# Four PSUM banks dealt anew, a batch's output scaled a slot earlier, and the probabilities turned in two halves

## The chip, the core and the metric

The kernel runs on one core of a Trainium2 chip. The metric is the device time of one execution in microseconds (us). The core's engines are TensorE (PE in the profile, its weight loads PEld), VectorE (DVE), ScalarE (ACT), GpSimd (POOL) and SyncE (SP), which issues nearly all transfers.

## The reference, cut to what matters

One step of a one-layer decoder trunk: 256 prompt tokens and 8 sequences (batches 0 to 7) of 8 new tokens, 320 columns in all.

```python
z = rmsnorm(x) @ w_in                    # 2048 -> 5120, split into q, k, v, u, h, gb, gc
# sample tokens, for each batch b: 8 queries x 16 heads against the cached keys (1280 of
# the 2048 positions are ever reached) and the 8 new ones, three dilated patterns merged
s = q @ k.T * HEAD_DIM**-0.5; s = where(valid, s, NEG)
p = exp(s - max(s)); o_att = (p @ v) / sum(p)
# prompt tokens: the same for 8 pairs of heads; besides it
h = associative_scan(exp(a*dt), u @ B); y = gelu(h @ C + D*u); y = y * sigmoid(y @ w_glu + b)
y_conv = gb * conv3(gc * h_in)
x = x + concat(rmsnorm(o_att), rmsnorm(y), rmsnorm(y_conv)) @ w_out
x = x + (silu(xn @ w_gate) * (xn @ w_up)) @ w_down     # xn = rmsnorm(x)
```

## The kernel before

All activations lie feature-major, [128 features, 320 tokens]. Each float32 weight is split into a high and a low part (`whi` by ScalarE, `wlo = raw - whi` by VectorE), and each product is made of three matmuls of 320 columns. The weights come in units of 512 KB, each 24 matmuls of TensorE.

The first 96 units (80 of `w_in`, then 16 of `w_out`) are the *slots* s = 0 to 95, and everything else of the layer is woven into them by slot numbers. On TensorE a slot is: the unit, with the calls of `middle(s)` inside it, then `end(s)`. On ScalarE and VectorE each slot holds, among other work, the split of unit s+2: ScalarE's copy waits for the end of unit s, so it begins where TensorE begins `end(s)`. Every engine runs its own list in order; what a slot's list holds late waits for what it holds early. After slot 95 only dense work is left, the loops over `w_gate`/`w_up` and `w_down` (from 587 us on).

Sample attention of batch b runs from slot START_OF[b] = 36, 42, 48, 54, 60, 66, 72, 78:

- slots +0 to +3: TensorE `scores(b, i)` into bank 6, at the end of the slot; VectorE `mask_scores(b, i)` adds the mask on the way into `sall` and takes the maxima. It stands ahead of VectorE's split of unit s+2 in the same slot.
- +4, +5: ScalarE spreads the maxima over the four groups of 32 partitions (`spread_maxima`, `spread_bias`, VectorE's `maxima` between them) and makes the exponentials of `sall` in place, groups 0 and 1 in slot +4, groups 2 and 3 in +5, with their sums in `psums`.
- +6 (TURN): VectorE `turn_probabilities(b)` transposes `sall` in 32x32 blocks into `ptk`, one instruction of 1408 elements a partition, after the ten value products of batch b-1 have read `ptk` (`v_used`). In slot +6 the scores of batch b+1 begin.
- +7 to +11 (VALUES): TensorE `values(b, j)`, ten products into bank 4, at the ends of the slots (1, 1, 1, 3 and 4 of them; two a slot for batch 7), and after the tenth `sum_probabilities(b)`, 4 tiny matmuls with the matrix `fold` that add the sums of the four partition groups.
- +11: VectorE `inverse_sums(b)`, a reciprocal out of bank 4.
- +12 (OUTPUT): ScalarE `scale_output(b)`: bank 4 times the reciprocal into `osb`, in its list behind the split of unit s+2. TensorE `turn_output(b)` waits for it and transposes `osb` back into bank 4, the last of the three kinds of work in `end(s)`: scores, values, turn. ScalarE `move_output(b)` takes the result away. Batches 0 and 1 (LATE) keep their output and turn it in slots 58 and 62, by way of bank 7.

Beside that: in slots 24 to 65 the state-space scan, 16 steps in 5 parts on VectorE. TensorE `project(i)`, in the middle of a slot, gives its input in two banks: 4 and 5 for i = 1, 3, 5, else 6 and 7. `read_out` takes four steps together into bank 5 (`y`, in slots 39, 50, 58 and 66), which VectorE's `scan_output` reads. In slots 66 to 82 there is prompt attention, a pair of heads in two slots: scores in banks 6 and 7 in the middle of the even slots (`prompt_masks` on VectorE), transposes into 6 and 7 at the end of the odd ones, values and output in bank 5. In 71 to 74 there are also the gate products in bank 5; slots 76 and 83 hold the sums of squares of two of the norms.

`fill(bank, key)` lets TensorE wait, ahead of each use of a bank, until the bank's last user in the order of the slots has been read. The function `fills(s)` writes that order down; for the banks of this change:

```python
def state_bank(i):
    return 4 if i < PAIRED and i % 2 else 6
...
"x": lambda: ("x_moved", key[1] + 1),
"score": lambda: ("s_masked", KS * key[1] + key[2] + 1) if key[2] < KS - 1 else ("new_masked", key[1] + 1),
```

So `project(10)` in slot 52 waits for the mask of batch 2's last scores (slot 51), `project(11)` in 55 for that of scores (3, 0), and `project(15)` in 63 for that of scores (4, 2), for all of them used bank 6.

Of the kernel before, what the change touches and what calls it, by code (L numbers as in the profile page):

```python
# [40 lines left out]
P = 128  # L41
# [169 lines left out]
def build(nc, a, o):  # L211
    with ExitStack() as ctx:
# [96 lines left out]
        psums = upper.take("psums", [P, DEC_BATCH, 4])  # L309
        fold = upper.take("fold", [P, 32])  # L310
# [36 lines left out]
        q_zero q_ready k_used s_masked s_max s_spread s_top s_bias p_exp p_turned new_masked fold_ready vn_zero  # L347
        p_sums s_sum v_used vn_done vn_moved
# [70 lines left out]
        def state_bank(i):  # L419
            return 4 if i < PAIRED and i % 2 else 6  # L420
# [14 lines left out]
        def fills(s):  # L435

            middle, end = [], []
            for i in range(ST):
                if scan_slot(i, 4) + 2 == s and i % 4 == 3:
                    middle.append((5, ("y", i // 4)))  # L440
            for i in projected(s):
                middle += [(state_bank(i), ("x", i)), (state_bank(i) + 1, ("x", i))]
# [22 lines left out]
            if s == VN_SLOT:  # L465
                end.append((7, ("vn", 0)))
            for b in range(LATE):
                if s == LATE_SLOTS[b]:
                    end.append((7, ("late", b)))
                if s == LATE_SLOTS[b] + 1:  # L470
                    end.append((7, ("turn", b)))
# [193 lines left out]
        def _(act):  # L665
# [70 lines left out]

            def exponent(b, groups):
                act.wait_ge(S["s_bias"], 4 * b + 4)
                for g in groups:
                    act.activation(sall[:, g, :], sall[:, g, :], ACT.Exp, bias=sbias[:, g:g + 1], scale=SCALE,  # L740
                                   accum_out=psums[:, b, g:g + 1]).then_inc(S["p_exp"], 1)
# [8 lines left out]
            def move_output(b):  # L750

                act.wait_ge(S["o_turned"], TURNS.index(b) + 1)
                bank = 7 if b < LATE else 4
# [48 lines left out]
            for s in range(SLOTS):  # L802
# [14 lines left out]
                for i in projected(s):  # L817
                    act.wait_ge(S["x_proj"], i + 1)
                    bank = state_bank(i)

                    if i > 1:
                        act.wait_ge(S["x_rot"], i - 1 if i <= PAIRED else i)
                    act.activation((xs if bank == 6 else xs_odd)[:], ps[:, bank:bank + 2, 0:NT], ACT.Copy).then_inc(S["x_moved"], 1)
# [42 lines left out]
                if s == VN_SLOT:  # L866
                    act.wait_ge(S["vn_done"], 1)
                    act.wait_ge(S["vn_zero"], 1)
                    for e in range(2):
                        act.activation(vn[0:64, 512 * e:512 * e + 512], ps[64 * e:64 * e + 64, 7, :], ACT.Copy).then_inc(S["vn_moved"], 1)  # L870
# [117 lines left out]
        def _(dve):  # L988
# [71 lines left out]
            def mask_scores(b, i):  # L1060

                if i == 0:
                    if b:
                        dve.wait_ge(S["p_turned"], b)
# [4 lines left out]
                v.tensor_tensor_reduce(out=sall[:, i, 0:KQ], in0=ps[:, 6, 0:KQ], in1=mask[:], scale=1.0, scalar=-3e38,  # L1069
# [9 lines left out]
                v.tensor_tensor(fresh, ps[own, 6, KQ:KQ + P].rearrange("p (a n) -> p a n", n=32), valid, ALU.add).then_inc(S["new_masked"], 1)  # L1079
# [15 lines left out]
            def turn_probabilities(b):  # L1095

                dve.wait_ge(S["p_exp"], 4 * b + 4)
                if b:
                    dve.wait_ge(S["v_used"], KEY_TILES * b)
# [4 lines left out]
                v.transpose(ptk[:].rearrange("p a n -> p (a n)"), sall[:].rearrange("p a n -> p (a n)")).then_inc(S["p_turned"], 1)  # L1104
                dve.wait_ge(S["p_turned"], b + 1)
# [3 lines left out]
            def inverse_sums(b):  # L1109
                dve.wait_ge(S["p_sums"], b + 1)  # L1110
                v.reciprocal(rsum[:, b:b + 1], ps[:, 4, 2 * P:2 * P + 1]).then_inc(S["s_sum"], 1)

            def scan(i, part):

                c_, s_ = (tab[:, i % 2, j:j + 1, :].to_broadcast([P, 2, NT]) for j in range(2))
                if part == 0:
# [3 lines left out]
                    x = xs if state_bank(i) == 6 else xs_odd  # L1120
# [43 lines left out]
            def scan_output(it):  # L1164
                dve.wait_ge(S["c_done"], 4 * it + 4)
                v.scalar_tensor_tensor(out=z[:, ZU + it, :], in0=z[:, ZU + it, :], scalar=vec[:, V_D + it:V_D + it + 1], in1=ps[:, 5, 0:NT],
# [66 lines left out]
            for s in range(SLOTS):  # L1233
# [24 lines left out]
                for b in batches(s, TURN):  # L1258
                    turn_probabilities(b)
# [72 lines left out]
                if s == START_OF[0] - 3:  # L1332
                    dve.wait_ge(S["early_done"], 1)
                    dve.wait_ge(S["ident_in"], 16)
# [858 lines left out]
```

## Time and profile before

| | us |
|---|---|
| median of 3 runs (lowest, highest) | 1539.41 (1535.3, 1539.87) |
| the profiled execution, its own time | 1536.41 |
| its span, first to last instruction | 1534.6 |
| busy: TensorE, VectorE, ScalarE, GpSimd | 1493.9, 842.2, 598.0, 218.6 |
| mean granted TensorE clock | 0.990 |

TensorE is busy for 97% of the span. Its matmuls are pipelined and their ends are modelled, so "busy" is not "at its peak". Times in the views are counted from the start of the span; a slot is about 5 to 9 us long in the stretch of slots 36 to 95, which lies between 141 and about 540 us.

### The profile page before, as it was taken

The page shows a single profiled execution, that of the slowest core. Times are in us where ns is not written, and L with a number is a line of the kernel's source. Part 1 is how long each engine was busy: PE and PEld are TensorE (multiplying, and loading weights), DVE is VectorE, ACT ScalarE, POOL GpSimd, SP SyncE. Part 2 cuts the span into 40 slices and gives each one's busy share as a digit, 9 for nine tenths or more (in the row PEclk, how much of TensorE's full clock was granted, in tenths as well). Part 3 has the DMA queues.
Part 4 walks back from the last instruction along what each step waited for, and adds up shares of the span by engine and source line. Part 5 has one row for each costly group of instructions (what it writes and reads, how often), then busy time and mean ns, then how long its engine had stood idle before and what let it go on. Part 6 is the DMA issues. An engine that isn't in the chain of part 4 may idle for free.

```text
span 1534.6 us, 27971 instructions
## 1 busy us (share of the span) xinstructions
PE 1493.9 (97%) x11431; PEld 1428.3 (93%) x11431; DVE 842.2 (55%) x1086; ACT 598.0 (39%) x883; POOL 218.6 (14%) x317
## 2 busy tenths in 40 slices
PE   9999998989989999999999999999999999999997
PEld 9998777778767899999999999999999999999997
DVE  7669899974467667544444444444444433333434
ACT  6333443437455354333333333333333433333332
POOL 7873344400440000000000000000000000000100
PEclk9999999999999999999999999999999999999999
DMA  7556798999779344444444444444444444444442
GB/s 265 190 168 220 277 377 308 346 338 372 270 262 369 125 152 151 146 147 148 148 150 150 150 150 150 149 146 147 148 149 150 151 151 151 151 144 152 145 152 109
DMA packets 93271, 296.41 MB, mean 193 GB/s; under 512 B 9728, under 2 KB 11008, under 8 KB 92800
## 3 DMA queue, kind: packets, MB, share of 16 engines
q1 hardware_dynamic: 92608, 294.10, 55.3%
q8 instruction: 63, 1.03, 0.3%
q10 hardware_dynamic: 576, 1.08, 0.2%
q14 instruction: 24, 0.20, 0.0%
HBM read 289.06 MB, written 5.43 MB: 192 GB/s over the span
## 4 chain that ended last, share of the span: by engine, by line
PE 84%; DVE 11%; ACT 3%; issue 2%; DMA 0%; SPq 0%; DVEq 0%; ACTq 0%
PE ps L2080 20%; PE ps L2079 20%; PE ps L2078 20%; PE ps L1924 5%; PE ps L1962 2%; PE ps L1926 2%; DVE wlo L1037 2%; PE ps L1968 2%; PE ps L1963 2%; PE ps L1775 1%; PE ps L1760 1%; PE ps L2029 1%; PE ps L2031 1%; PE ps L2030 1%; DVE tm L1122 1%
## 5 line engine op out<-in xcount | busy, mean ns | idle before, releaser
L1391 DVE TENSOR_TENSOR wlo<-raw,whi 128x1024 fp32r<-128x1024 f32 x264 | 325.3, 1232 | 519.9 <-ACT whi L914 519.7
L914 ACT ACTIVATE whi<-raw 128x1024 fp32r<-128x1024 f32 x264 | 279.9, 1060 | 606.2 <-PE ps L2080 601.7
L2080 PE MATMUL ps<-xh,wlo 128*128 128x320 f32 x1400 | 432.6, 309 | 0.0
L2078 PE MATMUL ps<-xh,whi 128*128 128x320 f32 x1400 | 432.6, 309 | 0.0
L2079 PE MATMUL ps<-xl,whi 128*128 128x320 f32 x1400 | 432.6, 309 | 0.0
L2078 PEld LDWEIGHTS ps<-xh,whi 128*128 128x128 f32 x1400 | 262.8, 188 | 0.0
L2079 PEld LDWEIGHTS ps<-xl,whi 128*128 128x128 f32 x1400 | 262.8, 188 | 0.0
L2080 PEld LDWEIGHTS ps<-xh,wlo 128*128 128x128 f32 x1400 | 262.8, 188 | 0.0
L2078 PE MATMUL ps<-hh,whi 128*128 128x320 f32 x696 | 215.1, 309 | 0.0
L2079 PE MATMUL ps<-hl,whi 128*128 128x320 f32 x696 | 215.1, 309 | 0.0
L2080 PE MATMUL ps<-hh,wlo 128*128 128x320 f32 x696 | 215.1, 309 | 0.0
L689 ACT ACTIVATE whi<-raw 128x1024 fp32r<-128x1024 f32 x110 | 116.2, 1057 | 188.8 <-PE ps L1924 89.6
L1037 DVE TENSOR_TENSOR wlo<-raw,whi 128x1024 fp32r<-128x1024 f32 x110 | 138.4, 1258 | 77.0 <-ACT whi L689 76.2
L1687 POOL TENSOR_TENSOR sq_last<-sq_last 128x1280 f32<-128x1280 f32 x2 | 5.9, 2972 | 1008.1 <-ACT sq_last L670 1008.1
L1924 PE MATMUL ps<-xh,whi 128*128 128x320 f32 x472 | 145.4, 321 | 0.0
L1926 PE MATMUL ps<-xl,whi 128*128 128x320 f32 x472 | 140.8, 311 | 0.0
L2079 PEld LDWEIGHTS ps<-hl,whi 128*128 128x128 f32 x696 | 130.7, 188 | 0.0
L2080 PEld LDWEIGHTS ps<-hh,wlo 128*128 128x128 f32 x696 | 130.7, 188 | 0.0
L2078 PEld LDWEIGHTS ps<-hh,whi 128*128 128x128 f32 x696 | 130.7, 188 | 0.0
L1924 PEld LDWEIGHTS ps<-xh,whi 128*128 128x128 f32 x472 | 89.4, 189 | 10.0 <-issue 7.7
L1962 PE MATMUL ps<-xh,whi 128*128 128x320 f32 x280 | 90.9, 332 | 0.0
L1926 PEld LDWEIGHTS ps<-xl,whi 128*128 128x128 f32 x472 | 89.6, 190 | 0.2
(336 smaller groups left out, 1836.7 us busy)
## 6 DMA issues: line engine op xcount, KB each, us to landing
raw<-in_w_gu SPq DMA_DIRECT2D x176, 512.0 KB, 3.3
raw<-in_w_dn SPq DMA_DIRECT2D x88, 512.0 KB, 3.3
raw<-in_w_in SPq DMA_DIRECT2D x78, 512.0 KB, 5.2
kv<-in_cv SPq DMA_DIRECT2D x64, 512.0 KB, 7.1
kv<-in_ck SPq DMA_DIRECT2D x32, 768.0 KB, 6.3
kv<-in_ck SPq DMA_DIRECT2D x32, 512.0 KB, 6.9
raw<-in_w_out SPq DMA_DIRECT2D x32, 512.0 KB, 3.4
raw<-in_cv SPq DMA_DIRECT2D x16, 512.0 KB, 7.8
```

The costliest lines, as they stand in the source:

```text
L689: act.activation(whi[:, u % SPL, :], raw[:, raw_place(u), :], ACT.Copy).then_inc(S["w_hi"], 1)
L914: act.activation(whi[:, j % SPL, :], raw[:, j % RAW, :], ACT.Copy).then_inc(S["w_hi"], 1)
L1037: v.tensor_tensor(wlo[:, u % SPL, :], raw[:, raw_place(u), :], whi[:, u % SPL, :].bitcast(F32), ALU.subtract) \
L1391: v.tensor_tensor(wlo[:, j % SPL, :], raw[:, j % RAW, :], whi[:, j % SPL, :].bitcast(F32), ALU.subtract) \
L1924: last = t_.matmul(ps[:, b0 + n, 0:NT], src[:, u % SPL, w], xh[:, k, :], start=False, stop=False)
L1926: t_.matmul(ps[:, b0 + n, 0:NT], whi[:, u % SPL, w], xl[:, k, :], start=False, stop=False)
L1962: t_.matmul(out, whi[:, u % SPL, w], xh[:, k, :], start=first, stop=False)
L1963: t_.matmul(out, whi[:, u % SPL, w], xl[:, k, :], start=False, stop=False)
L1968: last = t_.matmul(out, wlo[:, u % SPL, w], xh[:, k - 1 + kk, :], start=False, stop=j == units - 1 and kk == 1)
L2078: t_.matmul(out, whi[:, slot, w], ah[:, k, :], start=(k == 0), stop=False)
L2079: t_.matmul(out, whi[:, slot, w], al[:, k, :], start=False, stop=False)
L2080: last = t_.matmul(out, wlo[:, slot, w], ah[:, k, :], start=False, stop=(k == 2 * units - 1))
```

## The change

1. **Banks.** Scores go to bank 7 in place of 6. From i = 6 on the scan's input goes to banks 5 and 6 in place of 6 and 7. The second and third read-out (`y` 1 and 2, slots 50 and 58) go to bank 7, the others stay in 5. The new keys' and values' turn (`vn`) and the late batches' work go from bank 7 to 6.
2. **Sums.** `sum_probabilities`, its 4 matmuls a batch and `fold` are gone. In slot +7 ScalarE copies the four groups' sums side by side (`spread_sums`, 4 small copies); in +8 VectorE reduces them and takes the reciprocal; in +9 ScalarE deals the result out again (`deal_sums`, 4 small copies).
3. **Scaling.** `scale_output(b)` moves from slot +12 to +11, where it waits for the tenth value product of the same slot. In slot +12 `turn_output(b)` becomes the first work of `end(s)`, ahead of scores and values.
4. **Turn in halves.** VectorE transposes groups 0 and 1 at the end of slot +5 (after the exponentials of these two and `v_used` of batch b-1), ahead of the scan parts of that slot, and groups 2 and 3 in slot +6 in the place of the whole.

```diff
         def state_bank(i):
-            return 4 if i < PAIRED and i % 2 else 6
+            if i >= PAIRED:
+                return slice(5, 7)
+            return slice(4, 6) if i % 2 else slice(6, 8)
+
+        def y_bank(it):
+
+            return 7 if it in (1, 2) else 5
...
-                    end.append((6, ("score", b, step)))
+                    end.append((7, ("score", b, step)))
...
+            def spread_sums(b):
+
+                act.wait_ge(S["p_exp"], 4 * b + 4)
+                if b:
+                    act.wait_ge(S["s_sum"], b)
+                for j in range(4):
+                    act.activation(sums_at[0:32, j, :], psums[32 * j:32 * j + 32, b % 2, :], ACT.Copy).then_inc(S["p_sums"], 1)
+
+            def deal_sums(b):
+
+                act.wait_ge(S["s_sum"], b + 1)
+                for g in range(4):
+                    act.activation(rsum[32 * g:32 * g + 32, b:b + 1], sums_all[0:32, g:g + 1], ACT.Copy).then_inc(S["s_inv"], 1)
...
             def scale_output(b):
                 act.wait_ge(S["v_used"], KEY_TILES * (b + 1))
-                act.wait_ge(S["s_sum"], b + 1)
+                act.wait_ge(S["s_inv"], 4 * b + 4)
...
                 for b in batches(s, OUTPUT):
-                    scale_output(b)
                     if b >= LATE:
                         move_output(b)
+                for b in batches(s, VALUES + 4):
+                    scale_output(b)
...
+                for b in batches(s, VALUES):
+                    spread_sums(b)
+                for b in batches(s, VALUES + 2):
+                    deal_sums(b)
...
-            def turn_probabilities(b):
-
-                dve.wait_ge(S["p_exp"], 4 * b + 4)
-                if b:
-                    dve.wait_ge(S["v_used"], KEY_TILES * b)
+            def turn_probabilities(b, half):
+
+                dve.wait_ge(S["p_exp"], 4 * b + 2 * half + 2)
+                two = slice(2 * half, 2 * half + 2)
+                if half == 0:
+                    if b:
+                        dve.wait_ge(S["v_used"], KEY_TILES * b)
+                    v.transpose(ptk[:, two].rearrange("p a n -> p (a n)"), sall[:, two].rearrange("p a n -> p (a n)")).then_inc(S["p_turned"], 1)
+                    return
...
             def inverse_sums(b):
-                dve.wait_ge(S["p_sums"], b + 1)
-                v.reciprocal(rsum[:, b:b + 1], ps[:, 4, 2 * P:2 * P + 1]).then_inc(S["s_sum"], 1)
+
+                dve.wait_ge(S["p_sums"], 4 * b + 4)
+                if b:
+                    dve.wait_ge(S["s_inv"], 4 * b)
+                step(v.tensor_reduce(sums_all[0:32], sums_at[0:32].rearrange("p j g -> p g j"), AX.X, ALU.add))
+                v.reciprocal(sums_all[0:32], sums_all[0:32]).then_inc(S["s_sum"], 1)
...
                 for b in batches(s, 4):
                     maxima(b)
-                for b in batches(s, VALUES + 4):
+                for b in batches(s, VALUES + 1):
                     inverse_sums(b)
+                for b in batches(s, TURN - 1):
+                    turn_probabilities(b, 0)
...
             def end(s):
 
+                for b in batches(s, OUTPUT):
+                    if b >= LATE:
+                        turn_output(b)
...
-                for b in batches(s, OUTPUT):
-                    if b >= LATE:
-                        turn_output(b)
```

## Rows read from the trace of the kernel before

**Rows 1.** The page: the chain that ended last, by engine.
```profile
PE 84%; DVE 11%; ACT 3%; issue 2%; DMA 0%; SPq 0%; DVEq 0%; ACTq 0%
```

**Rows 2.** Waits of TensorE, whole span: total, times, longest, us.
```profile
PE ps L1800 <- ACT osb L748: 13.3, 6, 4.4
PE ps L1724 <- DVE smax L1069: 4.5, 2, 2.5
...
PE ps L1724 <- DVE sall L1079: 2.5, 1, 2.5
```

**Rows 3.** Busy us (instructions) by stretch: PE, PEld, DVE, ACT, POOL; clock, DMA share, GB/s.
```profile
130.00:257.00 127.00, 117.41 (x1225) 98.95 (x1225) 116.26 (x193) 51.84 (x123) 53.33 (x57) 0.99 0.84 301
257.00:286.00 29.00, 29.00 (x313) 22.75 (x314) 24.52 (x43) 9.81 (x21) 8.13 (x8) 0.94 0.86 320
286.00:312.00 26.00, 23.36 (x271) 19.15 (x270) 25.35 (x40) 12.20 (x37) 13.71 (x12) 1.00 0.96 353
312.00:333.00 21.00, 20.73 (x221) 16.45 (x221) 14.89 (x29) 8.38 (x24) 0.00 (x0) 0.92 0.87 323
333.00:378.00 45.00, 43.02 (x476) 35.49 (x474) 21.73 (x69) 26.37 (x71) 0.00 (x0) 1.00 0.97 365
```

**Rows 4.** Timeline of TensorE: start, duration, us; brackets: its idle time, and for what.
```profile
338.84 0.41 PE L1800 MATMUL ps<-ident,osb 128*128 128x128 f32 x2 [1.75 <-ACT osb L748]
...
386.39 0.41 PE L1800 MATMUL ps<-ident,osb 128*128 128x128 f32 x2 [2.54 <-ACT osb L748]
...
441.41 0.66 PE L1800 MATMUL ps<-ident,osb 128*128 128x128 f32 x2 [4.35 <-ACT osb L748]
...
484.18 0.41 PE L1800 MATMUL ps<-ident,osb 128*128 128x128 f32 x2 [2.06 <-ACT osb L748]
...
514.34 0.66 PE L1800 MATMUL ps<-ident,osb 128*128 128x128 f32 x2 [2.19 <-ACT osb L748]
```

**Rows 5.** TensorE alone by stretch: busy us, granted clock, DMA share, GB/s.
```profile
312.00:317.00 5.00, 4.73 (x35) 0.66 1.01 404
336.00:342.00 6.00, 4.25 (x54) 1.00 1.02 384
386.00:392.00 6.00, 5.61 (x30) 0.72 0.72 232
438.00:446.00 8.00, 4.59 (x24) 0.57 0.63 199
482.00:486.00 4.00, 1.95 (x14) 1.00 1.03 415
514.00:518.00 4.00, 3.66 (x16) 0.57 0.38 131
```

**Rows 6.** Timeline of TensorE and VectorE in slot 78.
```profile
435.77 1.29 PE L1760 MATMUL ps<-kv,qst 128*32 128x192 f32 x32 [1.68 <-issue]
...
436.14 0.08 DVE L1179 DVE_READ_ACCUMULATOR2_ANT pmax<- 128x1 f32 x1
```

**Rows 7.** Timeline of TensorE and VectorE in slots 47, 50 and 63.
```profile
204.64 1.93 PE L1775 MATMUL ps<-kv,ptk 128*32 128x256 f32 x32
...
224.59 1.29 PE L1760 MATMUL ps<-kv,qst 128*32 128x192 f32 x32
...
228.65 0.55 DVE L1166 SCALAR_TENSOR_TENSOR z<-z,vec,ps 128x320 f32<-128x320 f32 x1
...
312.27 1.04 PE L1724 MATMUL ps<-z,bt 32*128 32x320 f32 x4 [2.48 <-DVE smax L1069]
```

**Rows 8.** Small operations: duration ns min/median/max, first and last start us.
```profile
L1104 DVE STREAM_TRANSPOSE ptk<-sall x8: 1603/1641/1645, 178.1 to 481.6; 128x1408 f32<-128x1408 f32 x8
...
L1103 DVE STREAM_TRANSPOSE ptk_late<-sall x2: 313/314/314, 177.8 to 214.2; 128x128 f32<-128x128 f32 x2
...
L729 ACT ACTIVATE quads<-smax x32: 188/203/206, 167.4 to 472.2; 32x4 f32<-32x4 f32 x32
...
L1088 DVE TENSOR_REDUCE sbias<-quads x8: 158/163/170, 168.9 to 473.3; 32x4 f32<-32x16 f32 x8
```

More of the change, by code:

```diff
@@ L439, in fills @@
                 if scan_slot(i, 4) + 2 == s and i % 4 == 3:
-                    middle.append((5, ("y", i // 4)))
+                    middle.append((y_bank(i // 4), ("y", i // 4)))
             for i in projected(s):
-                middle += [(state_bank(i), ("x", i)), (state_bank(i) + 1, ("x", i))]
+                middle += [(bank, ("x", i)) for bank in range(8)[state_bank(i)]]
             for r in prompt_pair(s, 0):
@@ L465, in fills @@
             if s == VN_SLOT:
-                end.append((7, ("vn", 0)))
+                end.append((6, ("vn", 0)))
             for b in range(LATE):
                 if s == LATE_SLOTS[b]:
-                    end.append((7, ("late", b)))
+                    end.append((6, ("late", b)))
                 if s == LATE_SLOTS[b] + 1:
-                    end.append((7, ("turn", b)))
+                    end.append((6, ("turn", b)))
             return middle, end
@@ L752, in move_output @@
                 act.wait_ge(S["o_turned"], TURNS.index(b) + 1)
-                bank = 7 if b < LATE else 4
+                bank = 6 if b < LATE else 4
                 for e in range(2):
@@ L818, in _ @@
                     act.wait_ge(S["x_proj"], i + 1)
-                    bank = state_bank(i)
                     if i > 1:
                         act.wait_ge(S["x_rot"], i - 1 if i <= PAIRED else i)
-                    act.activation((xs if bank == 6 else xs_odd)[:], ps[:, bank:bank + 2, 0:NT], ACT.Copy).then_inc(S["x_moved"], 1)
+                    act.activation((xs_odd if i < PAIRED and i % 2 else xs)[:], ps[:, state_bank(i), 0:NT], ACT.Copy).then_inc(S["x_moved"], 1)
                 if s + 3 >= U_IN:
@@ L1119, in scan @@
                     dve.wait_ge(S["x_moved"], i + 1)
-                    x = xs if state_bank(i) == 6 else xs_odd
+                    x = xs_odd if i < PAIRED and i % 2 else xs
                     step(v.tensor_tensor(tm[:, 0:2], x[:], c_, ALU.mult), wait=False)
@@ L1258, in _ @@
                 for b in batches(s, TURN):
-                    turn_probabilities(b)
+                    turn_probabilities(b, 1)
                 for step_ in range(KS):
@@ L1720, in project @@
                 for plane, src in enumerate((z[:, ZU:ZU + NC, :], zr)):
-                    fill(state_bank(i) + plane, "x", i)
+                    bank = range(8)[state_bank(i)][plane]
+                    fill(bank, "x", i)
                     row = 32 * ((i + 2 * plane) % 4)
                     q = slice(row, row + 32)
-                    last = t_.matmul(ps[:, state_bank(i) + plane, 0:NT], bt[q, plane, i // 4, :], src[q, i // 4, :], start=True, stop=True,
+                    last = t_.matmul(ps[:, bank, 0:NT], bt[q, plane, i // 4, :], src[q, i // 4, :], start=True, stop=True,
                                      tile_position=(row, 0))
@@ L1759, in scores @@
                         for j in range(4):
-                            last = t_.matmul(ps[32 * j:32 * j + 32, 6, 64 * c0:64 * c1], qst[:, b % 2, 2 * i + half, :],
+                            last = t_.matmul(ps[32 * j:32 * j + 32, 7, 64 * c0:64 * c1], qst[:, b % 2, 2 * i + half, :],
                                              keys[:, :, half, :, j, :], start=(half == 0), stop=(half == 1), tile_position=(0, 32 * j))
                 last.then_inc(S["k_used"], 1)
-            def sum_probabilities(b):
-                pe.wait_ge(S["fold_ready"], 1)
-                pe.wait_ge(S["p_exp"], 4 * b + 4)
-                for g in range(4):
-                    last = t_.matmul(ps[32 * g:32 * g + 32, 4, 2 * P:2 * P + 1], fold[:], psums[:, b, g:g + 1], start=True, stop=True,
-                                     tile_position=(0, 32 * g))
-                last.then_inc(S["p_sums"], 1)
             def weigh(bank, turned, vals, start, stop):
@@ L1789, in values @@
                 weigh(4, ptk[:, :, 32 * j:32 * j + 32], kv_place(n), j == 0, j == KEY_TILES - 1).then_inc(S["v_used"], 1)
-                if j == KEY_TILES - 1:
-                    sum_probabilities(b)
             def turn_output(b):
-                bank, src = (4, osb) if b >= LATE else (7, osb_late[:, b, :])
+                bank, src = (4, osb) if b >= LATE else (6, osb_late[:, b, :])
                 if b >= LATE:
```

49 lines of the change are left out of this document (24 added, 25 removed).

## The prediction

> **What bounds the kernel now.** I read the page first. The chain that ended last runs over TensorE for 84% of the span and over VectorE for 11% [rows 1]. So time is to be had in two ways only: where TensorE stands idle or runs at its slow clock, and in the stretch where VectorE leads. Next I read the waits of TensorE [rows 2]. The largest by far is `osb`: six turns of an output wait for ScalarE's `scale_output`, 13.3 us in all. Three projections of the scan wait 4.5 + 2.5 = 7.0 us for VectorE's masks, because they share a bank with the scores. These four kinds of row are what the change is aimed at.
>
> Whether an idle microsecond is worth one depends on the stretch [rows 3]. From 130 to 257 us and from 286 to 312 VectorE is busy for 116.3 of 127 and 25.4 of 26 us: there VectorE paces, and TensorE's waits are TensorE waiting to be slow enough. From 257 to 286 and from 312 on it is the other way: TensorE is busy for 29.0 of 29 and 20.7 of 21 us, VectorE has 4.5 and 6.1 us free, and from 333 on about half. Five of the six `osb` waits lie in that late part, 1.75, 2.54, 4.35, 2.06 and 2.19 us long, 12.9 together [rows 4].
>
> The third thing read is the granted clock around these waits [rows 5]. Behind the wait that ended at 386.39 it averages 0.72 over 6 us, that is (1 - 0.72) x 6 x 2 = 3.4 us at 1.2 GHz instead of 2.4. Behind the ones at 514.34 and 312.27 it is 0.57 over 4 and 0.66 over 5 us: 3.4 us each too. Around 441.41 it is 0.57 over 8 us: 6.9 us slow, of which some 4 fall after TensorE goes on. Behind the waits of 1.75 and 2.06 us the clock stayed at 1.00. A slow stretch of 3.4 us does 1.7 us of work, so it costs 1.7 us more than the idle time in front of it.
>
> The Trainium skill's page "TensorE: Matmul & The Clock Gate", section "Part 1: The HAM clock gate", says that the slow clock is the default and that sustained activity releases it. The rows agree on the two levels.
>
> **The change part by part.**
>
> *Scaling a slot earlier, the turn first in its slot.* The product that `scale_output` needs is done at the end of slot +11, ScalarE scales it there, and the turn comes a whole unit later. All five late waits go. What ScalarE now waits for is `v_used`: it stands for at most the time of the value products less its own split copy. Behind it are queued the exponentials 2 and 3 of the next batch, which VectorE wants a slot later, and the prompt's probabilities, which come after the values in TensorE's list anyway. So I cost that wait at nothing, 0.5 us a batch if VectorE should be waiting. Gain 12.9 us. The clock: the stretches behind 386.39 and 514.34 go, 2 x 1.7 = 3.4 us.
>
> *What is late next, in slot 78.* There TensorE waits twice. Before the `osb` wait of 4.35 it stood 1.68 us at the scores, put down to "issue" [rows 6]; by the times this is VectorE's prompt masks (the fourth ended at 436.22 us; the second about 0.55 earlier, just before the scores' start at 435.77). Scores in bank 6 needed two of the masks; in bank 7 they need all four: +0.55. VectorE also makes the new first half of the turn in slot 77, ahead of the norm and of these masks: +0.9 (below). So this wait grows to about 3.1 us, 1.4 us lost, and at that length I expect the clock to fall behind it as it did behind 2.54, so the 2 us of slow work around 441 are not won. In the other even slots the fourth mask is done before the scores come, and I take 0; above 0.5 us each for five slots is the bound.
>
> *Halves of the transpose.* 1408 elements take 1641 ns, 128 take 314 [rows 8]: 1.037 ns an element and 181 ns fixed. A half of 704 costs 911 ns, two 1822: +0.18 us a batch. Between 0 (the fixed part hidden under its neighbour) and 0.36. Its wait for `v_used` of batch b-1 falls where VectorE is, by then, behind its split of the same slot; in the scan what is queued behind it are the scan parts and the next slot's masks.
>
> The page "VectorE: DVE Perf Modes" of the Trainium skill, section "The TRN2 errata", speaks against cutting an instruction up: a fixed cost is paid per instruction, some 150 cycles as it measured, which is 0.16 us by its clock. The rows give 0.18; by the page the halves would cost 8 x 0.16 = 1.3 us of VectorE's time in all instead of 1.4.
>
> *Sums.* VectorE: one more small reduce, 163 ns. ScalarE: 8 small copies of 203 ns, 1.6 us a batch; it has half of its time free from 333 on [rows 3], and the results are wanted two slots later: 0, or 1.6 us a batch if ScalarE led. TensorE loses 4 matmuls a batch; they lie in the gap it leaves anyway between tiled and full matmuls, so 0, at most 0.2 us each.
>
> *Banks, in the stretch to 333 us.* (a) The waits of projections 10, 11 and 15 go. Only the last lies where TensorE takes the lead: VectorE is free for 6.1 us after 312, so 2.48 us of idle time and 1.7 of slow clock come back: -4.2. The other two are worth something only between 257 and 286, where VectorE itself waited on TensorE: of its 4.5 us free there I take 2.5. (b) Read-out 1 now lies in bank 7, so scores (2, 2) must wait for `scan_output`. TensorE began them at 224.59; VectorE's `scan_output` ran at 228.65 to 229.20 [rows 7]. TensorE will stand for some 4.6 us, after which its clock falls. VectorE, which leads here, then waits for the scores (1.3 us long) before it can mask them, and about 1 us more in the next slot, since TensorE comes back at its slow clock: +2.3. (c) VectorE's 0.18 + 0.16 us for four batches: +1.4. Sum: -4.2 - 2.5 + 2.3 + 1.4 = -3.0.
>
> *Transfers.* None is added, but from 286 to 378 they run at a share of 0.87 to 0.97 and 323 to 365 GB/s; 404 and 415 GB/s over 4 to 5 us is the most the views show [rows 3, 5]. At 410 the 32.4 MB of these 92 us take 79 us, so the 5 to 6 us that I take out here fit, with bursts left over. I take 0.
>
> Sum: -12.9 - 3.4 + 1.4 - 3.0 = -17.9. The profiled execution took 1536.4, so 1518.5. The median of the runs stands 3.0 above that execution; I put half of it on: **1520 us**.
>
> **Rivals.**
>
> *A. The forecast.* 1520, its own range 1513 to 1527.
>
> *B. TensorE gains in the scan too.* If VectorE's lead is looser than its busy share says, the other two projection waits (4.5 us) and their slow stretches (3.4) come back in full: with the 2.5 already taken 1520 - 5.4 = about 1515, and with (b) unpaid as well 1512. Against it: 116 of 127 us busy.
>
> *C. Read-out 1 (and 2, slot 58) costs more.* TensorE stands 4.6 us with VectorE behind it, at the slow clock; if VectorE loses the whole of it, as much in slot 58, and 1.7 us of slow clock, that is 10.9 in place of 2.3: 1529. For it: VectorE leads there and every loss counts.
>
> *D. Something else is late in the prompt slots.* ScalarE's list or the transfers keep TensorE back where `osb` did. If the transfers give back all that is won up to 378 us, what is left are the four waits after it (11.1 us), their clock (3.4) and the 1.4 of slot 78: 1536.4 - 13.1 + 1.5 = 1525; if ScalarE's exponentials and table loads set slots 72 and 78, nothing much is left: 1536, no change. For it: 0.97 of DMA; against it: no wait for a transfer shows in the list.
>
> *E. Slower: VectorE blocked by the first half.* It waits for the ten value products of batch b-1, the last four of which take 1.93 us behind the unit [rows 7], about 2.3 with the new values' product; were VectorE always there early, that is 2.3 us of it a batch, and where a split or a mask behind it is late, as much for TensorE plus 1.7 us of clock: 4 x 8 = 32 us, 1520 + 32 = 1552. It decides once a batch loses 3.0 us of path (24 us in all). Against it: in the scan VectorE comes 2 us and more after the products, later it has half its time free.
>
> *F. The change doesn't do what it says:* the new scaling is itself late by a slot. It would need ScalarE a whole slot behind: 1539.
>
> **How the numbers follow.** Chances: A 0.50, B 0.08, C 0.14, D 0.16 (half of it with no gain), E 0.06, F 0.06. The range takes A, C, the better half of D and the nearer part of B: 1511 to 1532. A measurement here can tell 0.3%, 4.6 us, from no change. Faster: A + B + C + half of D = 0.80. Same: half of D and F with some of E's small end, 0.13. Slower: 0.07.
>
> **What would show it.** In the profile after: no wait of TensorE for `osb`, and the turn right behind each unit in slots 66 to 90; `scan_output` named as what scores (2, 2) wait for, 4 to 5 us, in slot 50; the wait at the scores of slot 78 grown to about 3 us; the granted clock at 1.00 around the turns of slots 72 and 90; two transposes of about 0.9 us a batch; VectorE at 312 us no earlier than 3 us before its old time. The forecast is wrong if VectorE's chain to 312 us grows by more than 3 us, or if a new row of ScalarE, VectorE or a transfer above 5 us appears among TensorE's waits.

## The result, and the profile after

The changed kernel takes 1517.03 us (median of 4 runs, 1515.17 to 1518.3), beside 1538.13 us for the kernel before on the same chip (4 runs, 1535.3 to 1539.87): a ratio of 0.9864, 95% interval 0.9844 to 0.9884. The forecast was 1520, its range 1511 to 1532. The profiled execution took 1515.17 us, its span 1513.3 at a mean clock of 0.997; before it was 1536.41 and 1534.6 at 0.990. So 21.2 us went, where the sum of the prediction had 17.9.

The page of the kernel after, the chain that ended last by engine, beside [rows 1]:

```profile
PE 85%; DVE 8%; ACT 3%; POOL 2%; issue 1%; DMA 0%; DVEq 0%; ACTq 0%
```

TensorE's waits in the kernel after (total, times, longest, us), beside [rows 2]:

```profile
PE ps L1793 <- DVE smax L1093: 4.1, 3, 1.8
PE ps L1793 <- DVE z L1198: 3.6, 1, 3.6
PE ps L1793 <- issue: 2.6, 1, 2.6
...
PE ps L1739 <- DVE sqc L1332: 1.6, 1, 1.6
PE ps L1770 <- DVE smax L1093: 0.9, 1, 0.9
```

No row of `osb` is left and none of a projection. What is new are four single waits: 3.6 us of scores for `scan_output` (`z`, slot 50), 2.6 us of scores in slot 78, 1.6 us of a norm's sums of squares in slot 83 (0.4 us before), and 0.9 us of read-out 1 in slot 50, which in bank 7 has to follow the mask of slot 49's scores.

Busy time by stretch in the kernel after (columns as in [rows 3]):

```profile
130.00:257.00 127.00, 116.95 (x1206) 98.30 (x1205) 114.52 (x188) 54.39 (x137) 52.13 (x53) 0.99 0.82 290
257.00:286.00 29.00, 29.00 (x323) 22.91 (x322) 27.98 (x54) 12.28 (x34) 11.17 (x12) 1.00 0.97 374
286.00:312.00 26.00, 26.00 (x299) 21.11 (x301) 25.37 (x40) 13.72 (x40) 13.19 (x12) 1.00 0.99 367
312.00:333.00 21.00, 21.00 (x241) 16.52 (x233) 17.84 (x44) 11.00 (x38) 0.00 (x0) 1.00 1.04 400
333.00:378.00 45.00, 44.90 (x475) 36.35 (x475) 21.41 (x70) 32.08 (x87) 0.00 (x0) 1.00 0.97 370
```

TensorE alone, in windows behind the five late turns and behind the two waits at scores (columns as in [rows 5]; the row from 428 begins 4.9 us behind slot 78's turn, the wait at the scores lies between them):

```profile
226.00:236.00 10.00, 6.38 (x62) 0.83 0.66 238
...
330.00:336.00 6.00, 6.00 (x71) 1.00 1.03 372
376.00:382.00 6.00, 6.00 (x65) 1.00 0.71 241
428.00:434.00 6.00, 6.00 (x72) 1.00 0.77 261
466.00:472.00 6.00, 5.77 (x49) 1.00 1.02 410
494.00:500.00 6.00, 6.00 (x43) 1.00 0.40 135
...
426.00:434.00 8.00, 7.99 (x113) 1.00 0.60 204
```

Between 257 and 286 us VectorE, which had 4.5 us free before, is now busy for 27.98 of 29: both engines are full. The clock, 0.94 and 0.92 in the second and fourth stretch before, is 1.00. TensorE stops for none of the five late turns, and the clock stays up behind them.

The scores of slots 50 and 78, and two of the turns, in the timelines of TensorE and VectorE after (start, duration, us; brackets: idle time before, and its releaser), beside [rows 4, 6, 7]:

```profile
229.51 0.55 DVE L1198 SCALAR_TENSOR_TENSOR z<-z,vec,ps 128x320 f32<-128x320 f32 x1
230.12 1.81 PE L1793 MATMUL ps<-kv,qst 128*32 128x192 f32 x32 [3.62 <-DVE z L1198]
231.97 0.49 DVE L1093 CUSTOM_DVE_ANT_0 sall<-ps,mask 128x320 f32<-128x320 f32 x1 [1.91 <-PE ps L1793]
...
330.46 0.38 PE L1822 MATMUL ps<-ident,osb 128*128 128x128 f32 x2
466.52 0.38 PE L1822 MATMUL ps<-ident,osb 128*128 128x128 f32 x2
...
425.84 0.08 DVE L1211 DVE_READ_ACCUMULATOR2_ANT pmax<- 128x1 f32 x1
426.01 1.29 PE L1793 MATMUL ps<-kv,qst 128*32 128x192 f32 x32 [2.56 <-issue]
```

The turns follow with no idle time in brackets. In slot 50 TensorE begins its scores 0.06 us after `scan_output` ends, at the slow clock (32 products in 1.81 us, not 1.29), and VectorE then waits 1.91 us for them. In slot 78 the scores begin 0.09 us after the fourth mask's maximum is read out (425.84 + 0.08), as the prediction had it; but behind this wait the clock is 1.00.

The small operations after (duration ns min/median/max, first and last start us), beside [rows 8]:

```profile
L1126 DVE STREAM_TRANSPOSE ptk<-sall x8: 899/905/911, 174.9 to 465.8; 128x704 f32<-128x704 f32 x8
L1132 DVE STREAM_TRANSPOSE ptk<-sall x8: 869/905/912, 179.1 to 466.7; 128x704 f32<-128x704 f32 x8
...
L1142 DVE TENSOR_REDUCE sums_all<-sums_at x8: 159/163/169, 191.2 to 480.1; 32x4 f32<-32x16 f32 x8
...
L750 ACT ACTIVATE sums_at<-psums x32: 187/203/205, 180.4 to 477.2; 32x4 f32<-32x4 f32 x32
L756 ACT ACTIVATE rsum<-sums_all x32: 182/200/203, 195.3 to 483.2; 32x1 f32<-32x1 f32 x32
```

To see where the 21 us went, one event that both kernels have is followed: the start of VectorE's `wlo` of each unit (unit s+2 is split in slot s). Each number below is such a start in the timeline, us. "Banks alone", "scaling late" and "no banks" are experiments 10, 1 and 4; "three edits" is experiment 9.

```
unit   before    after   banks   scaling    no    three
                         alone    late     banks  edits
  36   138.81   139.03   139.33   138.66   138.76  138.34
  51   221.44   222.30   221.97   221.92   222.01  220.91
  56   256.75   259.89   259.82   259.54   257.55  256.01
  59   277.32   276.18   276.46   275.83   276.05  272.35
  65   319.69   315.35   315.53   314.95   319.96  312.00
  68   338.37   333.13   333.62   333.16   338.61  329.78
  69   344.48   337.48   339.73   339.27   342.97  334.14
  74   385.92   378.82   380.73   380.61   384.77  375.46
  75   396.74   385.60   389.99   392.71   391.56  382.24
  80   439.51   429.00   432.62   436.10   435.10  424.24
  81   450.83   434.89   443.56   447.20   440.98  430.29
  83   464.98   448.70   457.59   461.23    455.12  444.10
  84   470.92   455.52   463.53   468.05   461.94  450.92
  90   503.44   486.01   496.05   500.55   492.46  481.91
  93   520.90   499.61   512.08   516.54   506.05  495.51
 110   581.37   560.09   572.55   577.01   566.53  555.98
```

The difference before to after grows in steps: +0.9 us at unit 51, +3.1 at 56 (slot 50), -1.1 at 59, -5.2 at 68 (slots 55 and 63), -7.0 at 69 (slot 66), -11.1 at 75 (slot 72), -10.5 at 80, -15.9 at 81 and -16.3 at 83 (all slot 78), back to -15.4 at 84 (slot 83), -17.4 at 90 (slot 84) and -21.3 at 93 (slot 90). From there to the end nothing changes.

One execution of a kernel differs from another, too. Kernels 2, 6, 7 and 8 below have the same instructions as after up to slot 48, and they reach unit 51 at 221.85, 221.76, 221.84 and 221.81 us, some 0.5 us sooner than after. A step of half a microsecond in this table is therefore not told from scatter.

### The profile page after: what moved, and what is told of

The parts are those of the page before. It is cut to its first block, busy times and chain, and to the rows that moved or that the text cites. A ratio compares the mean times of both kernels' runs of the same rounds, so it can differ in the third digit from the quotient of the medians.

```text
span 1513.3 us, 27929 instructions
## 1 busy us (share of the span) xinstructions
PE 1485.5 (98%) x11367; PEld 1419.5 (94%) x11367; DVE 841.6 (56%) x1101; ACT 609.5 (40%) x947; POOL 219.9 (15%) x317
## 4 chain that ended last, share of the span: by engine, by line
PE 85%; DVE 8%; ACT 3%; POOL 2%; issue 1%; DMA 0%; DVEq 0%; ACTq 0%
PE ps L2102 20%; PE ps L2100 20%; PE ps L2101 20%; PE ps L1946 5%; PE ps L1984 2%; PE ps L1948 2%; PE ps L1990 2%; PE ps L1985 2%; DVE wlo L1061 2%; PE ps L1799 2%; PE ps L1793 2%; PE ps L2053 1%; PE ps L2051 1%; PE ps L2052 1%; POOL par L1548 1%
```

## The experiments

All are made from the changed kernel; the baseline of each ratio is the kernel before on the same chip. Its median was 1538.13 us beside after, 1536.71 beside 1 to 4, 1535.98 beside 5 to 8 and 1537.14 beside 9 and 10, so medians of two of these groups compare only to 1 or 2 us; there the ratios and the starts of units are the better measure.

**1 and 2. The scaling back in slot +12, and the turn alone put last.**

```diff
 # 1, and in 2 this part is not made
                 for b in batches(s, OUTPUT):
+                    scale_output(b)
                     if b >= LATE:
                         move_output(b)
-                for b in batches(s, VALUES + 4):
-                    scale_output(b)
 # 1 and 2, in end(s): behind the scores and values, not ahead
                         if value_slot(b, j) == s:
                             values(b, j)
+                for b in batches(s, OUTPUT):
+                    if b >= LATE:
+                        turn_output(b)
```

> The changed kernel with one part undone: the scaling back in slot +12 and the turn last in its slot; banks, sums and halves stay. If the five late osb waits (12.9 us) and two slow stretches of the clock (3.4 us) are the core of the gain, they return in TensorE's waits and the time is 1517 + 16 = 1533, clock again 0.7 over the 6 us around slot 72's turn. Rival: banks and halves made the gain and the osb waits would only have moved elsewhere; then no more than 1521.

> Scaling in slot +11 as in the changed kernel, but the turn last in the slot again, behind scores and values. Theory: once the scaling is a slot ahead, the turn finds osb ready wherever it stands: 1517 within 1.5, no osb wait. Rival: the place of the turn matters by itself (more gaps between tiled and full matmuls, a later o_moved for bank 4): 1 us and more slower, at least 0.2 us in each of 6 slots.

Scaling late: 1533.91 us (10 runs), ratio 0.9978 [0.9968, 0.9987]. Turn last: 1516.98 us, 0.9875 [0.9858, 0.9892]. The first brings the waits back, in the list of TensorE's waits:

```profile
PE ps L1821 <- ACT osb L769: 12.6, 6, 3.6
```

So with everything else in place the scaling a slot earlier is worth 1533.91 - 1516.98 = 16.9 us of medians and 15.4 of the profiled executions (1532.09 - 1516.69). The turn's place in its slot is worth nothing that a median shows: an output scaled in time is turned without a wait wherever it stands. One thing in the second is odd. Its wait in slot 78 is 0.2 us longer than after's, and behind it the clock does fall. Timeline of TensorE, turn last:

```profile
425.96 1.32 PE L1793 MATMUL ps<-kv,qst 128*32 128x192 f32 x32 [2.77 <-issue]
```

and its window behind it:

```profile
426.00:434.00 8.00, 8.00 (x82) 0.79 0.60 202
```

It cost 1.25 us there (unit 81 at 436.14 against 434.89), most of the 1.5 us by which this execution is behind after's at unit 110 (561.59).

**3. The probabilities turned whole.** In slot +6, one instruction as before, and no first half in +5.

```diff
-                v.transpose(ptk[:, two].rearrange("p a n -> p (a n)"), sall[:, two].rearrange("p a n -> p (a n)")).then_inc(S["p_turned"], 1)
+                v.transpose(ptk[:].rearrange("p a n -> p (a n)"), sall[:].rearrange("p a n -> p (a n)")).then_inc(S["p_turned"], 2)
...
-                for b in batches(s, TURN - 1):
-                    turn_probabilities(b, 0)
```

> The changed kernel with the probabilities turned whole in slot +6 again. Theory: the halves only cost: 0.18 us of VectorE a batch, and 0.9 us ahead of slot 78's prompt masks. VectorE is 0.7 us sooner at 312 us, the wait at slot 78's scores falls from 2.56 to about 1.7, in all 1 to 2 us faster: 1515 to 1516. Rival: the halves bring VectorE's mask of slot +6 0.7 us sooner and so shorten TensorE's waits for masks (4.1 us in 3 rows): then 2 to 3 us slower, 1519 to 1520, with mask waits near 6 us.

1515.32 us (4 runs), 0.9865 [0.9848, 0.9881]; span 1513.4 against 1513.3. The time lies where a gain of 1 to 2 us was expected, but ratio and span show no gain. VectorE reached unit 51 at 221.20 instead of 222.30 (221.85 in kernel 2, on the same chip), and by unit 64 nothing of that is left: 310.98 against 310.99. The wait in slot 78 is 1.7 us, as before the change, and unit 81 starts 0.4 us sooner; at unit 90 that is gone as well (486.11 against 486.01). Both costs of the halves are there, and here neither reaches the end.

**4. The old banks.** `state_bank`, bank 5 for every read-out, scores in 6, `vn` and the late work in 7 again; the rest stays.

```diff
         def state_bank(i):
-            if i >= PAIRED:
-                return slice(5, 7)
-            return slice(4, 6) if i % 2 else slice(6, 8)
+            return slice(4, 6) if i < PAIRED and i % 2 else slice(6, 8)
         def y_bank(it):
-            return 7 if it in (1, 2) else 5
+            return 5
...
-                fill(7, "score", b, i)
+                fill(6, "score", b, i)
```

> The changed kernel with the banks as before (scores, projections and read-outs as they were). Theory: the waits of projections 10, 11 and 15 return with their slow clock, the 3.6 us wait for scan_output in slot 50 goes; the stretch to slot 66 ends about 4 us later than in the changed kernel, slot 78's wait is 0.55 shorter: 1517 + 4 = 1521. Rival: what the banks gained the read-out took back, and the banks are worth nothing: 1516 to 1518.

1521.57 us, 0.9902 [0.9885, 0.9919]. The projections wait again and `scan_output` is waited for by no one. TensorE's waits:

```profile
PE ps L1755 <- DVE smax L1091: 4.5, 2, 2.5
...
PE ps L1755 <- DVE sall L1101: 2.8, 1, 2.8
```

Everything but the banks is so worth 14.8 us by unit 110 (581.37 - 566.53), and in the scan nothing: unit 68 stands at 338.61 against 338.37 before.

This kernel also shows what the slow clock does to a step. Projection 11 waits 2.04 us before and 1.98 here. TensorE behind it, first before, then here:

```profile
257.00:262.00 5.00, 5.00 (x44) 0.66 0.93 356
```

```profile
257.00:262.00 5.00, 4.32 (x56) 1.00 1.03 371
```

From unit 56 to 59 before took 20.57 us, this kernel 18.50 and after 16.29: 2.2 us for the wait, 2.1 for the slow stretch that happened to follow it in one execution.

**5. The old sums.** `fold`, the four tiny matmuls and the reciprocal out of bank 4 in slot +11 come back; the scaling stays in +11.

```diff
-                for b in batches(s, VALUES + 1):
+                for b in batches(s, VALUES + 4):
                     inverse_sums(b)
...
-                for b in batches(s, VALUES):
-                    spread_sums(b)
-                for b in batches(s, VALUES + 2):
-                    deal_sums(b)
```

> The changed kernel with the sums as before: four tiny matmuls behind the tenth value product and the reciprocal on VectorE in slot +11, for which ScalarE's scaling in the same slot now waits. Theory: the moved scaling is what pays and the new sums only clear its way; VectorE makes the reciprocal 0.5 to 3 us after the products, ScalarE stands that long in slot +11, TensorE's turn is a slot later and doesn't see it: 1517 to 1519, no osb wait above 1 us. Rival: without the new sums ScalarE's list slips and w_hi or the exponentials come late: osb or mask waits of 1 us and more in several slots, 1522 and above.

1519.6 us, 0.9894 [0.9875, 0.9914]: between the two expectations. No wait for `osb` appears, so `scale_output` is in time even behind a reciprocal of the same slot. But ScalarE stands 1.42 to 2.94 us ahead of each of the six `osb` (at most 0.55 after), and its list slips; TensorE's waits:

```profile
PE ps L1788 <- ACT qst L730: 2.5, 3, 1.1
PE ps L1990 <- issue: 1.8, 1, 1.8
```

Against after this is 2.6 us of medians (1519.6 - 1517.0), on chips whose baselines differ by 2.1; by the ratios it is 4.6 us (0.0030 of 1537), by spans 4.7 (1518.0 - 1513.3). With the scaling early, the new sums are worth that, not by the matmuls they save but by letting ScalarE's list run. They have a price as well: slot 83's wait for `sqc` is 0.68 us here and 1.56 after.

**6 to 8. The two new waits taken away.** In 6 VectorE reads read-out 1 between two scan parts of slot 49, ahead of slot 50; in 7 the norm's steps come behind the prompt masks of slot 78; 8 is both.

```diff
 # 6
-                    if scan_slot(4 * it + 3, 4) + 2 == s:
+                    if scan_slot(4 * it + 3, 4) + 2 == s and it != 1:
                         scan_output(it)
...
                 for i, part in scan_parts(s):
                     scan(i, part)
+                    if (i, part) == (8, 1):
+                        scan_output(1)
 # 7
-                    normed(ZU, V_OUT + 12, rstd_s)
...
                 for r in prompt_pair(s, 0):
                     prompt_masks(r)
+                if s == SUM_SSM + 2:
+                    normed(ZU, V_OUT + 12, rstd_s)
```

> The changed kernel with scan_output(1) placed between two scan parts of slot 49 instead of in slot 50, nothing else. Theory: the wait of scores (2,2) for it, 3.6 us, set VectorE back by about 2.9 us; both go, VectorE is about 2.5 us sooner at unit 56, and since TensorE takes over from VectorE behind slot 55, 1 to 2.5 us of it last to the end: 1514.5 to 1516. Rival: VectorE leads with its own work and the wait cost nothing that counts: 1517, VectorE's split of unit 64 at its old time.

> The changed kernel with the norm's four multiplications (2.4 us of VectorE) behind the prompt masks of slot 78 instead of ahead of them. Theory: TensorE's wait of 2.56 us at the scores of slot 78, put down to issue, is for these masks; it goes to below 0.5 us, 2 us faster: 1515. Rival: the wait is for something else (bank 4, a transfer, ScalarE) and stays at 2 us and more: 1517, or the norm is now late for unit 80 and a new wait of up to 2 us takes its place.

> The edits of e6 and e7 together. Theory: they lie in different stretches and add up: 3 to 4.5 us faster than the changed kernel, 1512.5 to 1514. Rival: transfers (share 0.97 to 1.04 between 257 and 378 us in the changed kernel) hold what is won in the scan, and only e7's part is left: 1515.

| | median us | ratio, 95% interval | span |
|---|---|---|---|
| 6 read-out early | 1512.73 | 0.9852 [0.9833, 0.9872] | 1510.2 |
| 7 norm later | 1514.05 | 0.9861 [0.9841, 0.9881] | 1511.7 |
| 8 both | 1511.49 | 0.9843 [0.9824, 0.9863] | 1509.7 |

In 6 the row of `z` is gone and what slot 50 had cost is back for good: unit 56 at 256.90 (after: 259.89), unit 65 at 312.26 (315.35). Kernel 6 was 0.5 us ahead at unit 51 already, ahead of its edit, so the edit itself brings 2.5 us: as much as I expected at unit 56, and all of it stays. The median lies below the expected 1514.5 to 1516, but after's baseline stood 2.1 us higher: by ratios 6 is 1.8 us faster than after, by spans 3.1. In 7 the 2.6 us under "issue" are gone, which shows that they were the masks. At unit 74 kernel 7 was 1.0 us ahead of after already (377.77 against 378.82), which its edit, four slots later, can't have done; at unit 81 it was 1.6 ahead (433.28 against 434.89), so 0.6 of the 2.6 us are won. Kernel 8 says the same against 6: level at unit 74 (375.75 and 375.74), 0.55 ahead at 81. The rest comes up again one slot on, where the prompt's transposes wait for what is now late on VectorE. Timeline of TensorE, norm later:

```profile
422.78 1.29 PE L1794 MATMUL ps<-kv,qst 128*32 128x192 f32 x32 [0.39 <-issue]
...
432.70 0.52 PE L1847 MATMUL ps<-ident,sp 128*128 128x128 f32 x3 [1.75 <-DVE smax L1093]
```

**9. Both edits and the probabilities turned whole; 10. the banks alone.** 10 is the kernel before with part 1 of the change (besides, `psums` holds two batches in turn, not eight).

```diff
 # 9: the edits of 3, 6 and 7
 # 10: the edits of 1, 3 and 5; what is left against the kernel before:
-            return 4 if i < PAIRED and i % 2 else 6
+            if i >= PAIRED:
+                return slice(5, 7)
+            return slice(4, 6) if i % 2 else slice(6, 8)
...
-                    end.append((6, ("score", b, step)))
+                    end.append((7, ("score", b, step)))
```

> The change with three edits: read-out 1 taken up by VectorE between two scan parts of slot 49, the norm's eight small steps behind the prompt masks in slot 78, and the probabilities turned whole in slot +6. The first two together measured 1511.5. The theory that the halves are worth nothing expects 1511 to 1512.5 and the same list of waits. The rival, that the halves take work off VectorE's slot +6 where the prompt's transposes of slot 79 and the scores' masks want it, expects 1513.5 or more and a wait for smax that is longer than 1.8 us. The other rival, that their 0.18 us a batch of VectorE's time counts once the read-out is out of the way, expects 1510.5 or less, with unit 56 before 256.5 us.

> The kernel before with the banks of the change alone: the four tiny matmuls of the sums, the reciprocal in slot +11, the scaling in slot +12, the turn of the output last in its slot and the turn of the probabilities whole are as before. The theory that the parts add up takes the difference at unit 65 between the change and the kernel before, 4.3 to 4.6 us, as the banks' alone, and expects it kept to the end, since five osb waits remain where they were: about 1534 for a median of 1538 before, ratio about 0.997. It expects the wait of 3.6 us for scan_output in slot 50, no wait of a projection for the masks, and about 13 us of osb waits. The rival, that the new sums give back 1 us or more in the scan (their reduce and small copies on VectorE's and ScalarE's lists), expects unit 65 at 314.4 us or sooner instead of 315.3, and 1533 or less.

9: 1511.38 us (5 runs), 0.9836 [0.9823, 0.9849]; beside 8's 1511.49 no difference, as the theory had it. (The norm's steps that 7 to 9 move are four, not eight.) It is the fastest version with 8, and the plainer one. 10: 1528.37 us (6 runs), 0.995 [0.9935, 0.9965]: 5.6 us less than the theory said. That is below the rival's 1533 too, but not by the rival's way: unit 65 came where the theory had it (315.53), and the waits for `osb` are all there (12.8 us). Most of the extra came later, at the slow clock. The same wait of slot 72, scores done, turn waiting for `osb`, stands in three kernels, with a window of 6 us behind it (in the two below it begins 0.8 and 0.9 us after the wait's end). Before it was 2.54 us and the clock 0.72 [rows 4, 5]. Timelines of TensorE, first with the banks alone, then with the scaling late:

```profile
381.20 0.41 PE L1821 MATMUL ps<-ident,osb 128*128 128x128 f32 x2 [2.53 <-ACT osb L770]
```

```profile
381.08 0.66 PE L1821 MATMUL ps<-ident,osb 128*128 128x128 f32 x2 [2.52 <-ACT osb L769]
```

Windows of TensorE behind it, in the same order:

```profile
382.00:388.00 6.00, 6.00 (x40) 1.00 0.47 179
```

```profile
382.00:388.00 6.00, 6.00 (x28) 0.56 0.44 171
```

From unit 74 to 75 the four kernels took 10.82 (before), 9.26 (banks alone), 12.10 (scaling late) and 6.78 us (after, no wait). One wait of 2.5 us so cost 4.0, 2.5 or 5.3 us, in one execution each. In slot 90 it is the same: a wait of 2.19 us before with a clock of 0.57 behind it, one of 2.20 with the banks alone and 1.00. Timeline, then window, of TensorE, banks alone:

```profile
506.95 0.41 PE L1821 MATMUL ps<-ident,osb 128*128 128x128 f32 x2 [2.20 <-ACT osb L770]
```

```profile
506.00:512.00 6.00, 5.05 (x35) 1.00 0.25 87
```

## Why the prediction was right, and where its sum was off

Forecast A held: each of the prediction's steps is found in the trace, and the total is off by 3.3 us of the profiled execution (1518.5 against 1515.2). Term by term, the right column from the table of starts:

| step | predicted us | measured us |
|---|---|---|
| read-out 1 in bank 7 (slot 50, units 51 to 56) | +2.3 | +2.3 |
| VectorE's extra work in the scan | +1.4 | +0.9 by unit 51, about 0.5 of it scatter, then absorbed |
| projections 10 and 11 (units 56 to 59; 10 itself lies in slot 52) | -2.5 | -4.3 |
| projection 15 (units 59 to 68) | -4.2 | -4.1 |
| slot 66, wait of 1.75 | -1.75 | -1.8 |
| slot 72, 2.54 and its clock | -4.2 | -4.0 |
| slot 78, 4.35, less a longer wait at the scores | -2.95 | -5.4 |
| slot 83, `sqc` | 0 | +0.9 |
| slot 84, 2.06 | -2.06 | -2.0 |
| slot 90, 2.19 and its clock | -3.9 | -3.9 |

The right column adds up to 21.5, not 21.3, for it takes slot 78 from unit 80 to 81 alone. From unit 75 to 83, with the longer wait at the scores and a wait of 0.66 us in slot 77 (0.39 before), it is 5.1.

**Scaling a slot earlier.** Right: five waits gone, and the two slow stretches behind 386.39 and 514.34 with them. Experiments 1 and 2 put it at 15.4 (profiled executions) to 16.9 us (medians); predicted was 12.9 + 3.4 = 16.3. ScalarE's wait for the products cost nothing, as costed. "The turn first" is worth nothing by itself (experiment 2).

**Slot 78 is the first mis-sized term.** The prediction let the wait grow from 1.68 to about 3.1 us and the clock fall behind it, and therefore did not book the 2 us of slow work around 441. The wait grew to 2.56 and the clock stayed at 1.00. So about 4.35 - 0.9 + 2.0 = 5.4 us came back instead of 2.95 (5.1 by the starts of units 75 and 83). The step that failed is "at that length I expect the clock to fall": in one kernel it fell behind 2.77 us in this very place, in the other it did not behind 2.56, and experiment 10 has it not falling behind 2.53 where it had fallen behind 2.54. The length alone does not tell.

The wait in slot 50 goes further, for after, turn last (2) and norm later (7) have the same instructions up to it. It is 3.62 us long in all three. Timeline of TensorE in norm later, then the windows of 6 us behind the wait in after, turn last and norm later:

```profile
229.66 1.29 PE L1794 MATMUL ps<-kv,qst 128*32 128x192 f32 x32 [3.62 <-DVE z L1198]
```

```profile
230.12:236.12 6.00, 6.00 (x59) 0.72 0.56 177
```

```profile
229.66:235.66 6.00, 6.00 (x60) 0.76 0.41 131
```

```profile
229.66:235.66 6.00, 6.00 (x84) 1.00 0.61 208
```

So the clock behind a wait differs although neither the wait nor the work ahead of it does. The Trainium skill's page "TensorE: Matmul & The Clock Gate", section "Part 1: The HAM clock gate", says that the hardware sets the clock by how busy TensorE has been recently. The rows shown here agree in that each slow stretch stands in or behind a wait, but the list of instructions alone does not settle which wait has one. What decides, no run of this case shows. That after had no slow stretch in slot 78 was luck as far as these runs tell.

**The scan is the second.** The sum there was to be -3.0 and is -5.2 by unit 68. The slot 50 term is right in mechanism, place and size, although it came about a little otherwise: a wait of 3.62 us, not 4.6. Experiment 4, without the banks, has no such wait and stands level with the kernel before at unit 68, so all of this stretch's gain is the banks'. What was too small is the gain of projections 10 and 11. I took 2.5 of "VectorE's 4.5 us free" for the waits and nothing for the slow stretch behind projection 11, 257 to 262 us at 0.66, which is 1.7 us; only rival B names it. Between units 56 and 59 the gain was 4.3: 2.2 against experiment 4, which had the wait without the slow stretch, and 2.1 more. VectorE used nearly all that it had free, 27.98 of 29 us busy instead of 24.52. Its extra work, booked at 1.4, cost nothing in the end: experiments 3 and 4 stand within 0.3 us of their counterparts at units 64 and 68. It was paid into waits that VectorE had anyhow.

Both mis-sized terms are thus slow stretches and not waits: one that the prediction expected after the change and that did not come, one that had stood before the change and that the sum left out. The baseline carries the same chance: the kernel before took 1533.1 us in its fastest execution on record, at a mean clock of 0.993, and 1536.41 at 0.990 in the one that the prediction reads.

**The halves.** Their price is as worked out, 905 ns each, 0.17 us a batch more than 1641. They do lengthen slot 78's wait by 0.9 us (1.7 in experiment 3, 2.6 after), and still neither ratios (0.9865 and 0.9864) nor spans tell the kernels apart. The page "VectorE: DVE Perf Modes" of the Trainium skill, section "The TRN2 errata", which weighs against cutting an instruction up, is right here about the cost and silent on whether it is paid.

**The sums.** Costed at 0; with the scaling early they bring some 4.6 us through ScalarE's list (experiment 5), in which the 0.9 that they take back in slot 83 is counted. The prediction named neither. That the four matmuls cost TensorE next to nothing was right: from the last value products to the unit behind them it is 0.58 us before (507.78 to 508.36) and 0.54 after (490.36 to 490.90).

**The rivals.** B, more in the scan, is half true: projection 11's wait and its slow stretch came back, read-out 1 was still paid. C asked for 10.9 us from slots 50 and 58; only slot 50 stood, at 2.3 to 2.5. D: transfers at a share of 1.04 and 400 GB/s from 312 to 333 us, and no wait for one. E and F: no sign of either. (The chances beside them don't quite add: half of D with F is 0.14, not 0.13, and leaves 0.06 for slower.)

**The parts do not add.** Banks alone took 8.8 us by unit 110 (581.37 - 572.55), everything but the banks 14.8, together 23.6; the whole took 21.3. Of the banks' 8.8 some 3.0 are the slow stretches of slots 72 and 90 that happened not to come (10.82 - 9.26 and, from unit 92 to 93, 7.57 - 6.14), and the scaling takes away the same two.

Nor do the sums and the halves have a value of their own. With the scaling early the halves cost nothing and the sums bring 4.6 us. With it late, kernel 1 is kernel 10 plus just these two, and it is 4.5 us slower at unit 110 (577.01 against 572.55) and 5.5 in the median: 2.8 of that come in slot 72, where its wait had the slow stretch, 0.9 in slot 83 and the rest about slot 78.

## What to carry to other kernels

A short wait of TensorE has two prices, its length and perhaps a slow stretch behind it, and the second comes or goes from kernel to kernel and with the same instructions too: give it as a range, 0 to 1.5 us and once 2.8 here for a wait of 2.5, and don't read it as the gain of the part under test. Moving a consumer ahead of a busy engine's list is worth its full waits where the result can be had a slot earlier, while its place among the work of its own slot is worth nothing. When two users change banks, ask who now follows whom: the scores behind read-out 1 cost 2.5 us until its reader was moved up by a few instructions.

## What the runs showed of the hardware that I had not expected

Behind a wait of TensorE of nearly one length the mean granted clock came out anywhere from half to full: 1.00 behind 2.53 and 2.56 us, 0.79 behind 2.77, 0.72 behind 2.54, 0.56 behind 2.52 us; 0.57 behind 2.19 and 1.00 behind 2.20 us; 0.66 behind 2.04 and 1.00 behind 1.98; 0.72, 0.76 and 1.00 behind the same 3.62. These are means over 4 to 8 us that mix the two levels: before, the clock stayed full for some 1.4 us behind the wait of 2.54 and then fell to 1.2 GHz (0.50 from 388.4 to 390.4); with scaling late it stood at 0.50 for the whole 6 us behind 2.52.

In the three kernels with the wait of 3.62 us the instructions up to it are the same, so the edit does not decide it. The mean clock of the whole also changes from one execution of a kernel to the next: banks alone took 1526.9 to 1527.6 us in the three executions with a mean clock of 0.995 and 1529.1 to 1531.8 in the three with 0.992; scaling late took 1531.8 to 1532.2 at 0.992 and 1533.9 to 1534.5 at 0.990.
